# Seven half-size products in place of eight for the projections of a gated linear attention layer

## The reference

```
q, k, v, lr, z = split(rms_norm(x) @ w_in)          # per head: q 128, k 128, v 256, z 256 columns; lr 16 for all
lg = log_sigmoid(lr @ w_gate_up + gate_bias) / 16
S_new, o = blocked_scan(gla_block, S0, (q * 128**-0.5, k, v, lg))   # state 128 x 256 per head
x = x + (rms_norm(o) * silu(z)) @ w_out
```

## Time and profile before

| | |
|---|---|
| median of 3 runs | 3548.19 us (3547.81 to 3549.57) |
| profiled execution, first to last instruction | 3546.9 us |
| TensorE busy in it | 3479.6 us, 98% |
| VectorE, ScalarE, GpSimd busy | 33%, 31%, 14% |
| GLA stage with its 8 heads | from 2200 us to about 3140 us |

### The profile page before, as it was taken

How to read it: one execution, slowest core, us unless ns; L and a number is a source line. 1 busy time by engine, 2 the same in 40 slices (tenths; PEclk the granted TensorE clock), 3 DMA queues, 4 the chain that set the end, 5 groups by cost and what they waited for, 6 DMA issues and landing times. The chain is left out here.

```text
span 3546.9 us, 46800 instructions
## 1 busy us (share of the span) xinstructions
PE 3479.6 (98%) x16559; PEld 2561.4 (72%) x16559; DVE 1173.6 (33%) x2941; ACT 1101.9 (31%) x2810; POOL 513.4 (14%) x518
## 2 busy tenths in 40 slices
PE   8999999999999999999999998999999999999999
PEld 5777777776577778787766675677777777666676
DVE  2555555555233333333310233022222122220223
ACT  4334433343234343434210342122223122210242
POOL 1454444543000000000001002000000000011000
PEclk9999999999999999999999999999999999999999
DMA  5211130113311223112260102111111011371101
GB/s 159 50 39 38 32 30 27 35 32 103 92 37 46 42 45 44 42 29 87 95 214 30 36 24 75 36 30 45 39 51 45 24 44 39 123 229 48 36 1 49
DMA packets 245482, 205.99 MB, mean 58 GB/s; under 512 B 19904, under 2 KB 222432, under 8 KB 245320
## 3 DMA queue, kind: packets, MB, share of 16 engines
q1 hardware_dynamic: 239966, 194.29, 20.6%
q10 hardware_dynamic: 5360, 9.67, 0.7%
HBM read 157.95 MB, written 45.99 MB: 57 GB/s over the span
## 5 line engine op out<-in xcount | busy, mean ns | idle before, releaser
L510 PE MATMUL gdn_pj<-hT,Wb 128*128 128x352 f32 x1536 | 517.7, 463 | 5.4 <-ACT gdn_zraw L747 3.9
L2024 PE MATMUL gla_pj<-hT,Wb 128*128 128x352 f32 x1536 | 472.7, 462 | 6.9 <-PEq L45 6.3
L2024 PEld LDWEIGHTS gla_pj<-hT,Wb 128*128 128x128 f32 x1536 | 291.3, 191 | 157.6 <-issue 9.9
L1462 PE MATMUL band_pj<-hT,Wb 128*128 128x384 f32 (+1 forms) x1152 | 385.0, 463 | 4.9 <-ACT band_rs L1603 3.0
L510 PEld LDWEIGHTS gdn_pj<-hT,Wb 128*128 128x128 f32 x1536 | 266.9, 192 | 95.4 <-issue 4.9
L1462 PEld LDWEIGHTS band_pj<-hT,Wb 128*128 128x128 f32 x1152 | 206.4, 192 | 86.6 <-ACT band_rs L1603 7.1
L2020 PE MATMUL gla_pj<-gla_Wv,hT 128*128 128x256 f32 (+1 forms) x1152 | 266.8, 381 | 0.0
L2020 PEld LDWEIGHTS gla_pj<-gla_Wv,hT 128*128 128x128 f32 x1152 | 217.2, 190 | 31.8
L1648 ACT ACTIVATE band_E<-band_NS,band_nm 128x576 f32<-128x576 f32 (+9 forms) x136 | 89.7, 660 | 212.0 <-DVE band_nm L1726 211.9
L1216 POOL TENSOR_TENSOR x_kept<-gdn_AT,gdn_level 128x384 f32<-128x384 f32 x144 | 144.2, 1033 | 35.8 <-DVE gdn_TT L998 18.5
L1492 PE MATMUL band_pj<-Wb,hT 128*128 128x128 f32 x1152 | 144.2, 275 | 0.0
(11 more groups left out here) (417 smaller groups left out, 5452.9 us busy)
## 6 DMA issues: line engine op xcount, KB each, us to landing
Wb<-in_l_w_in_dram SPq DMA_DIRECT2D x96, 512.0 KB, 6.2
fin_xT<-x_features SPq DMA_DIRECT2D x16, 528.0 KB, 8.1
fin_R<-o_features SPq DMA_DIRECT2D x16, 528.0 KB, 9.4
Wb<-in_l_w_mkv_dram SPq DMA_DIRECT2D x8, 1024.0 KB, 5.4
Wb<-in_l_w_out_dram SPq DMA_DIRECT2D x16, 512.0 KB, 4.1
gla_Wv<-in_l_w_in_dram SPq DMA_DIRECT2D x8, 1024.0 KB, 5.3
o_features<-gla_OF ACTq DMA_DIRECT2D x14, 528.0 KB, 5.7
gdn_GB<-gate_rows SPq DMA_DIRECT2D x8, 544.0 KB, 3.6
```

The costliest lines, as they stand in the source:

```text
L510: mm = pe.matmul(pj[:, m % 2, 0:w], W[:, j, k, :], hT[:, k, c0:c0 + w], start=k == 0, stop=k == KD - 1)
L1462: mm = pe.matmul(out[:, 0:w], W[:, BAND_SLOT[j], k, :], hT[:, k, c0:c0 + w], start=k == 0, stop=k == KD - 1)
L2024: mm = pe.matmul(pj[:, m % 2, 0:w], W[:, SLOT[kind], k, :], hT[:, k, c0:c0 + w], start=k == 0, stop=k == KD - 1)
```

## The change

For z with its two halves, for q with k, and for v with its two halves, two 128-column projections are made as one product of 2 by 2 blocks. The blocks are: two halves of the features (4 of the 8 blocks each), two output columns of 128 (`A1`, `A2`), and two ranges of tokens (0 to 511, and 512 to 1055). Seven products of half the feature length replace the eight (a scheme of the Strassen and Winograd kind). Each pair of blocks runs in two units: all seven products on tokens 0 to 255 of both ranges, then on the rest (256 tokens of the first range, 288 of the second). One head has 3 pairs x 2 units x 7 products x 4 matmuls = 168 steps, as before; 120 have 256 columns and 48 have 288.

- P5, P6, P3 and P7 use sums of weights (`S4`), made by VectorE for each pair (`fast_weights`, four operations of 512 elements), and P6, P7 and P4 use sums of tokens (`TX`), made once at the start of the stage (`fast_tokens`). The token block in `hT` that they leave free is overwritten by the difference P3 needs.
- ScalarE copies P1, P5, P6 and P4 out of PSUM, VectorE adds P3, P7 and P2. P6 and P7 go on top of P1 in its bank, P3 on top of P5; so a product starts when the one two before it is out.
- Values are now made feature-major (`vT`) and turned by TensorE at the head's start: 18 transposes in five rounds (`turn_values`), each round copied to `V` by ScalarE (`values_out`). The copy `V<-vraw` goes, and the gate matmul now waits for these copies.
- The first head's values are still made in the old way, now as the first job of the stage.
- silu(z) moves on ScalarE from the head's start to behind step 40. The scale of q moves into `QG` on VectorE.
- VectorE's places are now those of `EVERY`; several buffers share room; the gate weights and the sample's state are loaded per head by SP, not copied by GpSimd. The first tiles of the residual now wait for the last turn of the values.

```diff
+SPLIT = 512
+WIDE = NTOK - SPLIT
+UNITS_OF = [(0, 256, 256), (256, 256, WIDE - 256)]
+FAST = ("P1", "P5", "P6", "P3", "P7", "P2", "P4")
+FAST_ACT = ("P1", "P5", "P6", "P4")
+FAST_DVE = ("P3", "P7", "P2")
+def fast_bank(unit, name):
+    c0 = unit[0]
+    return int(name in ("P5", "P3", "P2")) ^ int(c0 > 0)
+def fast_steps(pe, pj, left, right, unit, g, copied, added, done, operands):
+    for name in FAST:
+        w, bank = fast_width(unit, name), fast_bank(unit, name)
+        operands(name)
+        if name == "P1":
+            wait(pe, added, g * 3)
+        elif name == "P5":
+            wait(pe, copied, g * 4)
+        elif name in ("P6", "P3", "P7"):
+            pe.wait_ge(copied, g * 4 + {"P6": 1, "P3": 2, "P7": 3}[name])
+        else:
+            pe.wait_ge(added, g * 3 + {"P2": 1, "P4": 2}[name])
+        for k in range(FAST_K):
+            mm = pe.matmul(pj[:, bank, 0:w], left(name, k), right(name, k, unit[0], w),
+                           start=name in ("P1", "P5", "P2") and k == 0, stop=k == FAST_K - 1, skip_group_check=True)
...
+def fast_weights(dve, A1, A2, S4, i, made, q):
+    if i == 0:
+        dve.tensor_tensor(S4[:, 0, :, :], A2[:, 0:4, :], A2[:, 4:8, :], ALU.add).then_inc(made, 1)
...
 def head(h, more, turned=True):     # TensorE
-                    fill(lead)
-                    pe.wait_ge(picked, h * 2 + 2)
+                    if turned:
+                        for r in range(4):
+                            turn_values(h, r)
+                    fill(lead // 2)
+                    if turned:
+                        turn_values(h, 4)
+                    fill(lead - lead // 2)
+                    pe.wait_ge(picked, h + 1)
+                    pe.wait_ge(wg_ld, h * 16 + 16)
                     pe.wait_ge(lr_ok, 1)
                     wait(pe, o_fin, h * 6)
                     wait(pe, s_ok, h * TILES)
+                    if turned:
+                        pe.wait_ge(v_ok, h * 5)
...
 # VectorE, in head(h)
-                    dve.wait_ge(proj_out, h * NJ + NJ)
-                    wait(dve, o_done, h * TILES)
-                    wait(dve, p_done, h * TILES)
-                    dve.tensor_copy(V[:, :, :], vraw[:, :, :]).then_inc(v_ok, 1)
-                    adds(8)
-
+                    jobs(16)
                     dve.wait_ge(sp_ok, h * 3 + 3)
...
+                    jobs(20)
                     dve.wait_ge(lg_ok, h + 1)
...
+                    jobs(28)
                     dve.wait_ge(cb_ok, h + 1)
...
 # TensorE and SP, at the start of the stage and at its last head
+                first_values()
+                for i, _ in enumerate(project(0, 1)):
...
+                sp.wait_ge(v_turn, (H_C - 1) * 5)
                 for i in range(2):
                     early_x(sp, x_dram, x_stage, x_ld, i)
```

More of the change, by code:

```diff
@@ new lines, in _ @@
+                load_state(0)
+                sp.wait_ge(first_done, TILES)
+                load(1, "v")
+                for p in (1, 2):
+                    after(0, p)
+                    for kind in PARTS_OF[PAIR[p]]:
+                        load(1, kind)
+                head(0)
+                with sp.Fori(1, H_C - 2) as h:
+                    head(h)
+                n = H_C - 1
+                order = EARLY_ORDER[1]
+                sp.wait_ge(g_done, n)
+                load_gate(n)
@@ L2030, in head, with first_values @@
-                def head(h, more):
+                def first_values():
+                    pe.wait_ge(wv_ld, 16)
+                    pe.wait_ge(lr_ld, 16)
+                    for m, x in enumerate(FIRST_TILES):
+                        wait(pe, first_out, m - 1)
+                        for k in range(KD):
+                            mm = pe.matmul(pj[:, m % 2, 0:DV_C + RANK], hT[:, k, 128 * x:128 * x + 128], Wv[:, k, :],
+                                           start=k == 0, stop=k == KD - 1)
+                        mm.then_inc(first_done, 1)
@@ L2160, in head, with take @@
-                def head(h, more):
-                    left = list(range(NJ)) if more else []
+                def take(n, p, u, name):
+                    if u == 0 and name == "P1":
+                        if p == 0:
+                            act.wait_ge(v_turn, (n - 1) * 5)
+                        elif p == 1:
+                            wait(act, z_ok, n * 1)
+                        else:
+                            wait(act, qg_ok, n * 1)
+                            wait(act, kg_ok, n * 2)
+                    fast_copy(act, pj, target(p), UNITS_OF[u], units_before(n, p) + u, name, f_done, f_copy)
@@ L2162, in head @@
+                def head(h, more, turned=True):
+                    left = ends_of(FAST_ACT) if more else []
+                    left.sort()
                     LEAD, START, PER_GROUP, PER_TILE = EVERY
                     def jobs(steps):
[L2166 to L2171 removed]
@@ new lines, in head, with jobs @@
+                def head(h, more, last_projected=False):
+                    late = [] if more else list(range(len(EARLY)))
+                    lead, start, per_group, per_tile = EVERY if more else FINAL
+                    left = sorted(ends_of(FAST_DVE)) if more else []
+                    def jobs(steps):
+                        while left and left[0][0] <= steps:
+                            p, u, name = left.pop(0)[1:]
+                            take(h + 1, p, u, name, p < 2 or not last_projected)
@@ L2445, in early_steps @@
         if i < 2:
-            pe.wait_ge(*free)
+            for last in free:
+                pe.wait_ge(*last)
         else:
```

409 lines of the change are left out of this document (271 added, 138 removed).

## The result

The changed kernel takes 3494.82 us (median of 4 runs, 3491.63 to 3497.3) against 3548.0 us for the kernel before on the same chip: ratio 0.9848, 95% interval 0.9836 to 0.986. The forecast was 3494 us, range 3478 to 3518. The time, the sign and the main term came out; two terms of the sum were wrong in opposite directions, and the experiments are mostly about them.

A forecast was written before the change was run, and what follows sets the result against it. TensorE was taken to bound the kernel, busy 98% of the span. From 3546.9 us, -84.5 (work) + 6.6 (start) + 18.2 (head waits) + 4.8 (last head), plus 1.3 to the median, gave 3494 us; range 3478 to 3518.

The forecast's parts named there:

- TensorE's work, -84.5: GLA heads: fewer columns streamed, less the added transposes; 11.1 us off in each of seven heads, 7.0 in the first.
- The start, +6.6: Start of the GLA stage: first matmul now waits for the load of `Wv` and lr columns, 5.1 to 11.0 us.
- The slow first steps: Stage start: first steps run at granted clock 0.50 behind an idle; 2.6 us lost before and after alike.
- Waits in the heads, 2.6 each: Seven heads: TensorE waits for VectorE's additions at three places; 18.2 us in all, range 7 to 35.
- First and second wait: Each head: 0.7 us before P4, behind `lg`; 1.2 us before the next unit's P1, behind the running sum.
- the third, of 0.75: Each head: second unit's P2 waits 0.75 us for P3's addition, behind VectorE's operation held by `QS`, then `KK` and `KP`.
- it ends 2.92 later: Third wait: `QS` on GpSimd starts at 22.6 us and takes 2.92, holding VectorE's 32-element operation until 25.5.
- the check value of 98.5: One head from gate to gate should take about 98.5 us, where it was taken as 107.0.
- The last head, +4.8: Last head: gate 1.7 us later and a 3.1 us wait before the attention; range 2 to 8.
- the rival "the clock falls": Waits lower TensorE's clock in the heads: one fall per head gives 3512 us, three 3549; 5% in all.
- The other rivals: Waits mostly vanish, 3476 us, 8%; tiles not free, 3512, 14%; slow handover, 3584, 4%; change not done, under 1%.
- the handover: Each product's bank: eviction with semaphores takes 0.7 us, hidden; as rival over 1.72, with 2.0 giving 3584 us, 4%.

The follow-up runs named there:

- all_warm: The change plus VectorE's three early additions, last head's old addition order, ScalarE's DMA issues later, first load split, two unread matmuls before the last gate: 3474.09 us.
- warm: The change plus five matmuls with unread results in the last head, where TensorE waits for value copies and before the gate: 3490.68 us.
- the two lead kernels: As `all_warm` without its unread matmuls, but four or eight next-stage projection steps among the last head's turning matmuls: 3472.94 and 3476.45 us.
- again: The changed kernel run once more as it is: 3495.03 us, ratio 0.9851 to the kernel before.
- swap: The change with VectorE's 32-element operation set ahead of its 1024-element one: 3494.51 us, one run.
- last: The change with VectorE's early additions in the last head placed as before the change: 3488.16 us, ratio 0.9832 to the kernel before.
- order24: The change with P2's addition of the first unit ahead of VectorE's running sum: 3490.94 us.
- split: The change with the first load of the values' weights in four parts and the lr columns' load ahead: 3488.67 us.
- order_full: The change with P7's addition ahead of `lg`, P2's ahead of the running sum, P3's ahead of `KP`: 3485.24 us, ratio 0.9825 to the kernel before.

## Why the prediction came out right, and where it didn't

**TensorE's work, -84.5: right.** In the head shown a step of 288 columns took 1.94 / 4 = 0.485 us (2510.98 to 2512.92), as interpolated, 256 columns 0.431.

**The start, +6.6: right.** The load was issued at 2202.41, the first matmul came at 2208.89: 6.5. Cutting the load in parts, with the lr columns ahead, took 2.4 off, so it is the landing of these loads. The stretch to the first gate gained 2.4 for 1.7. The slow first steps don't go, but they cost less. TensorE, kernel before, then after:

```profile
2217.09 33.16 PE L2020 MATMUL gla_pj<-gla_Wv,hT 128*128 128x272 f32 x144
```

```profile
2208.89 34.91 PE L2190 MATMUL gla_pj<-gla_Wv,hT 128*128 128x272 f32 x144 [12.67 <-DMA gla_Wv<-in_l_w_in_dram]
```

The same 72 steps took 33.00 us from start to start before, where they came second, and 34.90 after, where they come first: 1.9 us lost, for 2.5 before (16.74 for 14.26, rows of 352 columns). That is 0.6 of the 0.7 us.

**Waits in the heads, 2.6 each: too high; 1.7 measured.** Six periods fell from 108.35 to 98.94 us, 9.4 each for 11.1 of work. First and second wait were 0.49 and 0.92 for 0.7 and 1.2, by the named instructions; the third, of 0.75, didn't come. The step that failed is "it ends 2.92 later". In this head `QS` took 2.04 us (2.01 to 2.13 in the seven heads; 2.92 in the last, where it began 0.97 us ahead of the 32-element operation, as before): it began as VectorE's 1024-element operation ended (2513.82 and 2513.99), while before it began ahead of that end. Part of the 2.92 was `QS` itself being held, and I took it for the length of the work. Of the rest of the 1.7, 0.3 a head, 0.1 is the product behind the second wait, which took 1.83 us for 1.73 (2509.15 to 2510.98); the other 0.2 I couldn't place.

**A misreading that cost nothing.** The period of a head before was 108.35, not 107.0: the window of the earlier trace rows begins 3.4 us behind the gate's start (2516.30), and I took its left edge for the gate's end. Only the check value of 98.5 rests on it; 108.35 - 11.1 + 2.6 would have been 99.9, measured 98.9.

**The last head, +4.8: too low; 11.2 + 1.6 measured.** The waits came as worked out: 3.08 us for 3.1; in front of the gate 1.11 + 1.40 in place of 0.91, 1.6 more for 1.7. What failed is the step against the rival "the clock falls": from one wait of 0.80 without a loss I concluded that waits this short cost only themselves. That rival was given 5% for one fall per head. It was true of the one head that I hadn't asked it about, where two waits stood within 2 us behind 22 transposes and another of 3.1 us followed: 8.0 us. In the seven other heads the waits are as I said, the granted clock is 1.00, and they cost themselves.

So 3494 for 3494.8 is in part luck: 7 x 0.9 = 6 us and 0.7 at the start too pessimistic, 8 too optimistic. The other rivals fell: no product but those named waits, and the handover costs nothing once the order is right.

**Open.** What exactly lowers the clock in the last head. Shown: it falls behind the change's two waits in all seven kernels that have both; filling them with matmuls kept it up; with no waits and the values' transposes and gate matmuls together it still fell for a while (`all_warm`); with four or eight long steps among these it didn't. So neither waits nor short matmuls alone decide. A difference that no run separates: `warm` and the two lead kernels have long matmuls ahead of the last two transposes as well as behind them, `all_warm` has them only behind. The DMA traffic doesn't decide alone: from gate to ten rows on, the DMA engines were as busy before (1.00, 355 GB/s from 3054.15 to 3064.30) at a granted clock of 1.00 as after the change at 0.52. How far the clock falls differs between kernels that are the same in that stretch: gate and ten rows took 10.2 to 10.3 us in the change, `again`, `swap` and `last`, 8.7 in `order24` and `split`, 7.05 in `order_full`, for 5.35. Their gates start at different times, between 2984.20 and 2990.95, but `again` and `order24`, whose gates are 0.2 us apart, differ by 1.6 us too. What decides it, these runs don't tell.

## What to carry to other kernels

When the bound engine gets less work per unit, walk the queues of the engines that evict it with their long instructions, and put evictions ahead of them: three one-line moves gave back 6 us. Look separately at the last pass of a loop, where no next work fills the gaps: here it cost 13 us of a gain of 67. And compare stretches by landmarks, since in three of these runs a third or more of the time gained had nothing to do with the edit.

## What the hardware showed beyond expectation

- A wait of 3.08 us on TensorE cost 6.4 in all in the change: the instructions behind it ran at a granted clock of 0.62 (mean of 3021.70 to 3030.00) and took 8.0 us for 4.84. In five other kernels the same wait cost 4.9, the instructions behind it taking 6.61. The Trainium skill, "TensorE: Matmul & The Clock Gate", section "A second HAM failure mode: psum-queue depth-cycling", speaks of a clock that goes up and down with short idles. The last head of the change agrees with it; the seven heads with waits of 0.49 and 0.92 us don't, their granted clock is 1.00, and in `all_warm` it fell with no idle over 0.2 us.
- GpSimd's two-operand operations and VectorE's operations with two SBUF operands ran one after the other, not slower side by side. 1088 elements on GpSimd took 2.04 us where it began as such an operation of VectorE ended, and 2.92 where it began with 0.97 us of one still to run; VectorE's took 2.00 for 0.19 (32 elements) and 2.38 for 0.69 (512) beside it. The same befell one of the new sums of weights in a head, beside the scaling of the outputs. GpSimd, then VectorE, in the kernel after:

```profile
2553.28 1.48 POOL L2645 TENSOR_TENSOR gla_OR<-gla_OR,gla_rs 128x768 f32<-128x768 f32 x1 [37.41 <-ACT gla_rs L2447]
```

```profile
2553.46 1.84 DVE L1942 TENSOR_TENSOR gla_S<-gla_S,Wb 128x512 f32<-128x512 f32 x1
```

That sum takes 0.69 in the median of its 16. It is what the prediction held in its upper end from the Trainium skill, "GPSIMD Engine Reference", section "1. Specifications", and it delayed no product. The 138 additions that read PSUM took 0.38 to 0.46 us, without exception; seven of them ran beside a scaling on GpSimd, and took 0.42.
